# A hybrid decoder step on one NeuronCore: turns by token moved between the projections, Pool's sample update in eight parts, another order of loads and stores

## What is computed

```python
h = rms_norm(x, norm_mix)
proj = h @ w_in                                  # 1024 x (1792 + 768)
# group A, RWKV-7: token shift, LoRA decay / rate / gate, then per token
S = S * w_t + (S @ a_t) b_t^T + v_t k_t^T ; y_t = S @ r_t      # 8 heads x 64 x 64
y_rwkv = (group_norm(y) + bonus) * g
# group B: sliding-window attention (128), 8 query and 2 key/value heads, rotary, sinks
x = x + concat(y_rwkv, y_swa) @ w_out
x = x + cross_attention(rms_norm(x, norm_cross), memory K/V of 256 rows)
x = x + moe(rms_norm(x, norm_ffn))               # 4 groups x 8 experts, top-1 group, top-2 experts
return rms_norm(x, norm_final), new shift rows, states, window and memory caches
```

## Time and profile before

| | |
|---|---|
| runs before, us | 875.69, 880.60, 880.22 (median 880.22) |
| profiled execution, us | 877.09, of which 875.0 from the first to the last instruction |
| mean granted TensorE clock | 0.874 of full speed |
| TensorE busy, us | 705.6 (81%) |
| VectorE busy, us | 371.0 (42%) |
| ScalarE busy, us | 214.0 (24%) |
| GpSimd busy, us | 87.1 (10%) |
| transfers | 113.88 MB, mean 130 GB/s |

### The profile page before, as it was taken

The page is one execution under the profiler, slowest core; times in us unless marked ns, Lnnn a source line. Parts: engine busy times, 40 slices in busy tenths (PEclk is TensorE's granted clock), DMA queues, the critical chain, the costliest instruction groups (busy, mean ns, idle before and its releaser), DMA issues.

```text
span 875.0 us, 16008 instructions
## 1 busy us (share of the span) xinstructions
PE 705.6 (81%) x6960; PEld 539.6 (62%) x6960; DVE 371.0 (42%) x717; ACT 214.0 (24%) x536; POOL 87.1 (10%) x80
## 2 busy tenths in 40 slices
PE   3999999999658898657898989858795439999930
PEld 3874887888658788546753448645345337777710
DVE  3310149980545655754483230463241542222208
ACT  4250114333312122344501111331111002222213
POOL 0100000002570000000000000000000013444210
PEclk9999999999887999957988999975996559999965
DMA  7722240000210000220407020023448537999825
GB/s 260 271 97 96 97 145 1 0 1 27 87 50 4 3 4 4 102 53 1 173 27 288 1 96 1 25 96 78 170 155 307 212 130 295 408 406 405 315 99 216
DMA packets 42490, 113.88 MB, mean 130 GB/s; under 512 B 10187, under 2 KB 12677, under 8 KB 41116
## 3 DMA queue, kind: packets, MB, share of 16 engines
q1 hardware_dynamic: 37556, 104.31, 32.1%
q0 software_dynamic: 4864, 8.53, 2.7%
HBM read 105.88 MB, written 16.24 MB: 140 GB/s over the span
## 4 chain that ended last, share of the span: by engine, by line
PE 64%; DVE 18%; ACT 5%; DMA 5%; POOL 3%; issue 3%; SPq 2%; POOLq 0%; DVEq 0%; ACTq 0%
PE bank L844 47%; PE bank L1457 7%; PE bank L1471 4%; PE bank L848 3%; PE bank L1443 2%; DMA hn_d<-arena 1%; DVE arena L1853 1%; DMA vec_d<-arena 1%; PE bank L1465 1%; ACT arena L1614 1%; DMA arena<-hn_d,arena 1%; DVE arena L2034 1%; DVE arena L1899 1%; ACT arena L1631 1%; DVE arena L1926 1%
## 5 line engine op out<-in xcount | busy, mean ns | idle before, releaser
L844 PE MATMUL bank<-arena 64*64 64x64 f32 (+12 forms) x5160 | 529.0, 299 | 61.8 <-DVE arena L1972 11.2
L844 PEld LDWEIGHTS bank<-arena 64*64 64x64 f32 (+5 forms) x5160 | 400.2, 162 | 178.7 <-issue 86.8
L848 PE MATMUL bank<-arena 128*128 128x128 f32 (+5 forms) x392 | 58.7, 303 | 61.4 <-issue 16.6
L848 PEld LDWEIGHTS bank<-arena 128*128 128x128 f32 (+5 forms) x392 | 50.8, 170 | 76.9 <-issue 27.5
L1457 PEld LDWEIGHTS bank<-arena 128*64 128x64 f32 x1024 | 58.6, 138 | 19.8 <-issue 19.8
L800 POOL DMA_INDIRECT arena<-hn_d,arena x16 | 16.7, 1046 | 475.3 <-DVE arena L2238 450.8
L1457 PE MATMUL bank<-arena 128*64 128x128 f32 x1024 | 63.5, 276 | 0.0
L2245 DVE TENSOR_TENSOR arena<-bank,arena 128x512 f32<-128x512 f32 x32 | 22.1, 692 | 59.8 <-PE bank L1443 59.8
L1553 ACT COPY arena<-bank 128x260 f32<-128x260 f32 x40 | 15.0, 376 | 110.3 <-PE bank L844 110.3
L1648 ACT COPY arena<-bank 128x256 f32<-128x256 f32 x56 | 20.9, 373 | 79.7 <-PE bank L844 78.5
L804 POOL DMA_INDIRECT pair_d<-arena x32 | 31.8, 994 | 60.7 <-ACT arena L1742 54.0
(11 more groups left out here) (232 smaller groups left out, 540.9 us busy)
## 6 DMA issues: line engine op xcount, KB each, us to landing
arena<-in_w_exp_gate SPq DMA_DIRECT2D x32, 512.0 KB, 10.5
arena<-in_w_exp_up SPq DMA_DIRECT2D x32, 512.0 KB, 14.1
arena<-in_w_exp_down SPq DMA_DIRECT2D x32, 512.0 KB, 15.0
arena<-in_w_in SPq DMA_DIRECT2D x5, 2048.0 KB, 9.4
arena<-in_x_prompt SPq DMA_DIRECT2D x8, 512.0 KB, 5.3
arena<-in_w_out SPq DMA_DIRECT2D x2, 2048.0 KB, 10.9
arena<-in_cache_mem_k SPq DMA_DIRECT2D x8, 512.0 KB, 7.1
arena<-in_cache_mem_v SPq DMA_DIRECT2D x8, 512.0 KB, 3.7
```

What stands on the lines that cost most here:

```text
L844: last[0] = pe.matmul(out, lhsT, rhs, start=start, stop=stop, skip_group_check=True)
L848: last[0] = pe.transpose(out, in_, ident[0:n, 0:n])
```

## The change

The rows that TensorE turns by token move from after projection 19 to between projection 17 and the last two, which now run half by half (18 and 19 on the first 260 tokens, then both on the rest). Bonus and reciprocals of VectorE move with them. GpSimd's scaling waits for the first halves only, for its first eight blocks. The sample vectors are staged in another place, so that their store to DRAM goes out at once, and the copies of the sample window caches come behind them in SP's queue. GpSimd's six long operations are cut into eight parts each. VectorE's first sample step moves behind tile 0's `fin`, the second into tile 2, behind `Y` of tile 1. At the start x, the identity and the first gain are loaded first. The stores of the normed rows to `hn_d` are issued by ACT. In the tail the register is read before the waits, the sample rows go first, and tile 0 is combined by TensorE: three products with the identity and two diagonal matrices for each half, copied out by ACT.

```diff
 FRONT_ORDER = [...
-               ("proj", 11), ("proj", 16), ("proj", 17), ("proj", 18), ("proj", 19)]
+               ("proj", 11), ("proj", 16), ("proj", 17), ("turn", 0), ("last", 0), ("last", 1)]
-RECUR_ORDER = [("tok", 0, 0), ("AB", 0, 0), ("AB", 0, 1), ("N0", 0, 0), ("level", 0, 0), ("level", 0, 1),
-               ("sample", 0, 0)] + [("level", 0, k) for k in range(2, 6)] + [("fin", 0, 0)]
+RECUR_ORDER = [("AB", 0, 0), ("AB", 0, 1), ("N0", 0, 0), ("level", 0, 0), ("level", 0, 1)] + \
+              [("level", 0, k) for k in range(2, 6)] + [("fin", 0, 0), ("sample", 0, 0)]
 for _t in range(1, TILES):
-    RECUR_ORDER += [("tok", _t, 0), ("U", _t - 1, 0)] + [("sample", 0, 1)] * (_t == 1) + \
+    RECUR_ORDER += [("tok", _t, 0), ("U", _t - 1, 0)] + \
         [("AB", _t, 0), ("S", _t - 1, 0), ("AB", _t, 1), ("U", _t - 1, 1), ("N0", _t, 0), ("level", _t, 0),
-         ("S", _t - 1, 1), ("level", _t, 1), ("Y", _t - 1, 0)]
+         ("S", _t - 1, 1), ("level", _t, 1), ("Y", _t - 1, 0)] + [("sample", 0, 1)] * (_t == 2)
...
# SP, start
+            sp.dma_start(x[:, 0, :], A["x_prompt"][0, 0:P, :]).then_inc(s_x[0], 16)
+            sp.dma_start(ident, c[:, 0:P]).then_inc(s_first, 16)
+            for t in range(1, TILES):
+                sp.dma_start(x[:, t, :], A["x_prompt"][0, t * P:(t + 1) * P, :]).then_inc(s_x[t], 16)
+            load_gain(0, "norm_mix", s_first)
+            sp.dma_start(x[0:NS, 4, :], A["x_sample"][:, 0, :]).then_inc(s_x[4], 16)
+            load_first(0)
+            sp.dma_start(srow[0:NS, :], A["state_rwkv_shift"][0]).then_inc(s_par, 16)
...
# SP, handover
+            done(sp, ("svec", 5))
+            sp.dma_start(vec_d.rearrange("a b n -> b a n"), svt6).then_inc(s_svd, 16)
             done(sp, ("shift_out", 3))
...
             sp.wait_ge(s_svd, 16)
+            sp.wait_ge(full, place[("proj", 19, 1)] + 1)
...
# GpSimd
             for n in range(NCH):
+                if n % 4 == 0:
+                    pool.wait_ge(full, place[("proj", 19, n // 4)] + 1)
...
-            tt(Stmp, SS, a_, ALU.mult).then_inc(s_sa, 1)
-            link(tt(SS, SS, w_, ALU.mult))
+            for p in parts:
+                tt(Stmp[:, p, :], SS[:, p, :], along(0), ALU.mult).then_inc(s_sa, 1)
+            for p in parts:
+                tt(SS[:, p, :], SS[:, p, :], along(3), ALU.mult).then_inc(s_pch, 1)
             pool.wait_ge(s_ssa, 1)
-            link(tt(Stmp, b_, ssa.unsqueeze(2).to_broadcast([P, 32, HD]), ALU.mult))
...
+            for p in parts:
+                tt(Stmp[:, p, :], along(1), across(ssa, p), ALU.mult).then_inc(s_pch, 1)
+            for n, p in enumerate(parts):
+                pool.wait_ge(s_pch, 9 + n)
+                tt(SS[:, p, :], SS[:, p, :], Stmp[:, p, :], ALU.add).then_inc(s_pch, 1)
...
# TensorE, start: the turn of parameters and shift rows comes behind that of x
-            pe.wait_ge(s_par, 16 * 14)
+            pe.wait_ge(s_first, 32)
...
# TensorE, "turn": svec, tokV, shift_out, tok of tile 0
+            def turned_by_token():
+                pe.wait_ge(s_prep, 4)
+                pe.wait_ge(s_mix, 14)
...
# VectorE, in "turn"
+                    done(dve, ("tokV", 3))
+                    for c in range(4):
+                        V_ = PR[:, 8 + c, 1:1 + NT]
+                        tt(V_, V_, yT[:, c, :], ALU.mult).then_inc(s_bv, 1)
...
                     if t == 0 and n == 0:
                         dve.wait_ge(s_mask, 5)
+                        dve.wait_ge(s_shout, 32)
+                        dve.wait_ge(s_svd, 16)
...
# ACT, in the cross output (SP's stores and its wait for them are gone)
+            def rows_written(t):
+                R = tile_rows(t)
+                act.wait_ge(s_xn2, 6 + t)
+                act.dma_start(hn_d[t * P:t * P + R, :], xn[t % 2][0:R, :]).then_inc(s_hn[t % 2], 16)
...
                 elif step not in ("cpT", "coT"):
+                    if step > 0:
+                        rows_written(step - 1)
                     row_norm("wc", step)
+            rows_written(TILES)
...
# tail: SP
+            beyond = sp.value_load(eidI[0:1, OVER:OVER + 1], min_val=0, max_val=OVER)
+            sp.wait_ge(s_pY, NE)
             for i in range(NB3):
                 sp.wait_ge(s_ys[i], 16 * (NE // NB3))
...
-            for t in range(T5):
+            for t in (TILES,) + tuple(range(TILES)):
...
# tail: TensorE
+            pe.wait_ge(s_diag, 1)
+            pe.wait_ge(s_yl[0], 16)
+            for n, o in enumerate((banks[2], banks[6])):
+                cols = slice(n * 512, (n + 1) * 512)
+                mm(o[:, :], ident, x[:, 0, cols], True, False)
+                for j in range(2):
+                    mm(o[:, :], diag[j], ydt[0][:, j, cols], False, j == 1)
+                last[0].then_inc(s_pC, 1)
# tail: ACT takes the tiles in the order 4, 1, 0, 2, 3 and copies both halves of tile 0 to x
# tail: VectorE
-            combined(0)
-            for t in range(1, T5):
-                combined(t)
-                final_rows(t - 1)
-            final_rows(T5 - 1)
+            combined(TILES)
+            combined(1)
+            final_rows(TILES)
+            combined(2)
+            final_rows(1)
+            final_rows(0)
+            combined(3)
+            final_rows(2)
+            final_rows(3)
```

More of the change, by code:

```diff
@@ L90 @@
 WC_ORDER = ("csT", 0, "cpT", 1, "co", 2, "coT", 3, 4)
+FINAL_ORDER = (4, 1, 0, 2, 3)
 def tile_rows(t):
@@ L115, in bank_plan @@
             g += [(("proj", n, s), "a") for s in range(2)]
+        elif what == "last":
+            g += [(("proj", j, n), "a") for j in (18, 19)]
         elif what == "mT":
@@ L694, in _ @@
                 load_expert(i, i, s_wgu[i], s_wd[i])
-            for t in range(T5):
[L697 to L701, removed]
-                sp.wait_ge(s_xn2, 6 + t)
-                sp.dma_start(hn_d[t * P:t * P + R, :], xn[t % 2][0:R, :]).then_inc(s_hn[t % 2], 16)
+            done(sp, ("coT", 1))
+            for i in range(2, 5):
+                load_expert(i, i, s_wgu[i], s_wd[i])
             sp.wait_ge(full, place[("wc", 4, 1)] + 1)
@@ L871, in _, with project @@
                     close()
-            def project(j):
+            pe.wait_ge(s_par, 16 * 12)
+            o = reuse(pe, ("par",))
+            tr(o[:, 0:42], prow[0:42, :])
+            close()
+            o = reuse(pe, ("shift_in",))
+            for j in range(RW):
+                tr(o[:, NS * j:NS * j + NS], srow[0:NS, j * P:(j + 1) * P])
+            close()
+            def project(j, halves=(0, 1)):
                 grp = j // 4
@@ L877, in project @@
                 w = weights(key)
-                for s in range(2):
+                for s in halves:
                     o = reuse(pe, ("proj", j, s))
@@ L939, in _ @@
                     project(n)
+                elif what == "last":
+                    project(18, (n,))
+                    project(19, (n,))
                 elif what == "mT":
@@ L1566, in memory, with rows_by_token @@
                 return act.copy((mkS if name == "mk" else mv)[:, t, :], o[:, :])
+            def rows_by_token(t):
+                for i in range(3):
+                    o = filled(act, ("tok", t, i))
+                    act.copy(tokXs[t % 2][i], o[:, :]).then_inc(evac["a"], 1)
             for what, n in FRONT_ORDER:
@@ L1570, in _ @@
                     from_psum([("proj", n, s) for s in range(2)], projected)
+                elif what == "last":
+                    from_psum([("proj", j, n) for j in (18, 19)], projected)
                 elif what == "lora_in":
@@ L1639, in _ @@
                 elif what == "tok":
[L1640 to L1642 removed]
+                    rows_by_token(t)
                 elif what == "level":
@@ L1755, in _ @@
                 act.wait_ge(s_pY, NE)
-            for t in range(T5):
+            combined = 0
+            for t in FINAL_ORDER:
                 R = tile_rows(t)
-                act.wait_ge(s_comb, t + 1)
+                if t == 0:
+                    for n, o in enumerate((banks[2], banks[6])):
+                        act.wait_ge(s_pC, n + 1)
+                        link(act.copy(x[:, 0, n * 512:(n + 1) * 512], o[:, :]))
+                else:
+                    combined += 1
+                    act.wait_ge(s_comb, combined)
                 ms = small[0:R, t:t + 1]
```

204 lines of the change are left out of this document (97 added, 107 removed).

## The result

| | before | after |
|---|---|---|
| median, us (runs) | 877.96 (4) | 848.01 (4) |
| lowest to highest, us | 874.80 to 880.60 | 847.35 to 850.28 |
| profiled execution, us | 877.09 | 848.17 |
| mean granted clock | 0.874 | 0.889 |

The ratio is 0.966, with a 95% interval of 0.963 to 0.968. Forecast were 853 us and a range of 845 to 863. The two profiled executions are 28.9 us apart, their spans (875.0 and 846.0) 29.0.

A forecast was written before the change was run, and what follows sets the result against it. TensorE, holding 64% of the chain, was taken to bound the kernel. From 877.1 us, start -3.9, handover -14.6, stores -6.5 and tail -0.3 gave 851.8, or 854.9 on the median's scale; forecast 853 us, range 845 to 863.

The forecast's parts named there:

- Start (-3.9): Kernel start: loading x first brings the first projection, and everything behind it, sooner; -3.9 us, bounds 0 and -5.4.
- rival of a start bound by bytes: Kernel start: the first gain or the weights come no sooner; +3.9 us, 857, chance 0.10.
- Cover for the bonus (-3.7): Handover: VectorE's bonus runs under four projection halves, so masking of AB begins sooner; -3.7 us, bounds 0 and -4.6.
- Step 1 out of the levels and tile 0's clock (-1.7, -1.8): Handover, tile 0: TensorE's 1.70 us wait goes, -1.7 us; a shorter gap holds the upper clock level, -1.8 us.
- Step 2 out of tile 1's start (-9.0): Handover, tile 0 to 1: 17.96 us shrink to 9.0, judged by 8.08 in tile 1 to 2; -9.0 us.
- Step 2 in tile 2 (+2.1): Tile 2, behind Y: 4.6 us of VectorE's work meet 2.50 us of idle time, delaying level 2's sum; +2.1 us.
- Tile 1's clock (-1.0): Tile 1's start: a gap of 2.4 us instead of 10.11 may spare the clock; -1.0 us, 0 to -1.8.
- GpSimd in parts (0): Handover: 48 parts cost 26 to 52 us and end between 262 and 279, so step 2 needn't wait; 0 us.
- rival "the turns cool the clock": Handover: transposes don't count for the clock gate, so turns and projections run partly at half speed; +5.7 us, chance 0.08.
- Stores (-6.5): Ahead of routing: issued by ACT, the store lands before VectorE needs it; -6.5 us, 0 to -6.5.
- rival "routing keeps the upper level": Routing products: the upper clock level is kept as VectorE's gap shrinks; up to -7.5 us, 845.5, chance 0.07.
- Tail (-0.3): Kernel end: earlier register read and TensorE combining tile 0, against a larger last store; -0.3 us, -3 to +2.

The follow-up runs named there:

- Experiment 4: The changed kernel with VectorE's four bonus products made to wait for the last projection half: 853.7 us, +5.7 against the changed kernel.
- Experiment 11: The changed kernel with VectorE's second sample step done twice in tile 2: 854.3 us, +6.3 against the changed kernel.
- experiment 2: The changed kernel with GpSimd's six sample operations whole again instead of eight parts each: 854.9 us, +6.9 against the changed kernel.
- experiment 3: The changed kernel with the five stores of normed rows to hn_d back on SP's queue: 852.8 us, +4.8 against the changed kernel.
- experiment 8: The changed kernel with five additional identity products in TensorE's 2.9 us wait ahead of the routing products: 848.7 us, +0.7 against the changed kernel.
- experiment 7: The changed kernel with tile 0 combined by VectorE instead of TensorE, order sample rows, tiles 1, 0, 2, 3: 851.8 us, +3.7 against the changed kernel.
- experiment 1: The changed kernel with both of VectorE's sample steps back at their old places: 867.4 us, +19.4 against the changed kernel.
- experiment 10: The changed kernel with ACT's table loaded early, the first gain ahead of x's second tile, and TensorE waiting for the identity alone: 849.2 us, +1.2.
- experiment 9: The changed kernel with the routing products of tiles 0 to 2 ahead of the turns of the sample rows: 843.7 us, -4.3 against the changed kernel.

## Why the prediction was right

- **Start (-3.9).** Right in its mechanism and in its size: 4.1 at the first projection (24.37 to 20.28), 4.3 at the turns between kernels that both show the dip of the clock. The two profiled executions show 2.4 because that of before has no dip. The prediction had no term for the clock here; it carried the shift of the first projection through to the end unchanged. The rival of a start bound by bytes falls.
- **Cover for the bonus (-3.7).** AB to first level went from 7.79 to 4.44 us: -3.35. Experiment 4 takes it back at 3.5.
- **Step 1 out of the levels and tile 0's clock (-1.7, -1.8).** From the first level to the first `fin` copy lie 15.06 us instead of 19.14: -4.1 for -3.5. The clock is 1.00 throughout (222.3 to 238).
- **Step 2 out of tile 1's start (-9.0).** From the end of the last `fin` copy to tile 1's first level 9.08 us instead of 17.96: -8.9. This was the largest term, and the method behind it, taking the undisturbed next tile as the measure, is what carried the forecast.
- **Step 2 in tile 2 (+2.1).** Wrong: it cost 0 (tile 2's first level to tile 3's takes 33.42 us, before 33.40). The step that failed is the reading of VectorE's idle time in one bracket (2.50 us) as all the slack there is; TensorE had other products queued, and the sums that were 1.9 us late at 294.7 were on time at 298.7. Experiment 11 shows that the slack is hardly more than the 4.6 us used.
- **Tile 1's clock (-1.0).** Didn't come: the clock is at 0.53 for 3.5 us behind the wait of 2.58, much as in tile 2. The gain is 0.2 (22.28 us for tile 1's long run of products instead of 22.50).
- **GpSimd in parts (0).** The time of a part was right (0.58 to 0.76, between the bounds of 0.54 and 1.09), and nothing waited for it. Yet that nothing waits for GpSimd's chain is only half of what the cut does: VectorE's operations beside GpSimd wait for the end of an instruction, 0.2 to 0.9 us with parts or 4 to 6 with whole ones. Left whole at the new places, the operations would have eaten 5 to 7 of the 16.5 us (experiment 2). The sum had no such term, for better or worse; it came out right because the change did cut them, which is luck as far as the reasoning goes. The collisions with parts, for which the prediction has +0.5, lengthen VectorE's operations (0.62 for 0.41, 1.60 for 0.75); what of that reaches TensorE no run shows. The rival of a high fixed cost falls.
- **The rival "the turns cool the clock".** Falls: 1.00 from 196.5 to 218 through 7.37 us of transposes. The rule of the Trainium skill ("TensorE: Matmul & The Clock Gate", Part 4), by which transposes don't count, cost nothing here.
- **Stores (-6.5).** Exactly so between the two traces; 5.2 in experiment 3. The rival of a store that is late from ACT's queue too falls.
- **Routing (0).** Right: 14.93 us as before. The rival "routing keeps the upper level" falls twice, by the trace and by experiment 8.
- **Tail (-0.3).** Under-estimated by 2.5. The register's read gives 0.9 (0.8 forecast). TensorE took 7.09 us for tile 0 instead of 10.5, because the clock rose to 1.00 3.3 us after it started (at 829.1); so VectorE never waited the 2.2 us for it, and the whole 2.5 us of the two operations are gained, as experiment 7 shows. VectorE's other wait, for tile 1's rows, is there (2.62 us for about 2). The last store costs 0.9 instead of 1.1.

Two misses make the kernel faster than the sum (+2.1 that didn't come, 2.5 more in the tail) and one slower (1.5 at the start, the dip); together they make most of the 3.6 us between 851.8, the sum, and 848.2. That the total is this near is thus in part because they offset each other.

## What to carry to other kernels

Where a step must wait for a slow engine, place it where the waiting engine's next user has slack, and price the place by the same stretch of an undisturbed iteration; that slack is finite, and doubling the step shows where it ends. What one edit is worth can hang on another: the parts make GpSimd's chain 5.5 us longer, which costs nothing only because the steps have moved, and the moved steps lose 5 to 7 us of their gain without the parts. Before a stage's gain is taken from two single traces, look whether a stretch that the change doesn't touch has the same clock in both.

## What the runs showed of the hardware

- An elementwise operation of VectorE with both inputs in SBUF waits for the end of GpSimd's running instruction (4.19 us in place of 0.41, and 6.93 in place of 0.75 for two). Beside GpSimd's parts it got in quickly (0.62; 1.60 for two), but in experiment 1 not for 13.35 us and some twenty parts, until GpSimd had ended. What decides between the two is open.
- In all thirteen traces of the changed kernel or an edit of it the clock falls to 0.50 for 3 to 7 us, beginning 8 to 16 us after TensorE's first work, whether its turns leave gaps or not, and at another moment each time. Only the trace of before has no such dip.
- Ahead of the dip, TensorE's first turns run at about half speed while the clock column says 1.00 (1.94 us for eight at 7.20 in experiment 10, 1.15 at 14.07 in the changed kernel).
- The routing products (36 columns) lose the upper clock level 1.8 and 4.2 us after they start, though TensorE doesn't stop (experiments 8 and 9); transposes of 128 columns, 7.37 us in a row, keep it.
